# Prompt attention in pairs of query blocks, with split probabilities and values and a third probability buffer

## What is computed

```
def fox_attend_block(q, cq, qpos, k, v, ck, kpos):
    s = jnp.einsum('nqhd,nkhd->nhqk', q, k).astype(jnp.float32) * (FOX_HEAD_DIM ** -0.5)
    bias = jnp.swapaxes(cq, 1, 2)[..., :, None] - jnp.swapaxes(ck, 1, 2)[..., None, :]
    mask = kpos[None, :] <= qpos[:, None]
    p = jax.nn.softmax(jnp.where(mask, s + bias, -jnp.inf), axis=-1)
    return jnp.einsum('nhqk,nkhd->nqhd', p.astype(v.dtype), v)
```

## Time and profile before

| | |
|---|---|
| time, 3 runs | 1847.37 us median (1846.79 to 1848.72) |
| the profiled execution | 1848.54 us, its span 1846.5 us |
| PE busy over the span | 97% (PEld 93%) |
| DVE, ACT, POOL busy | 55%, 28%, 42% |
| granted PE clock, mean | 0.995 of 2.4 GHz |

### The profile page before, as it was taken

The page is one execution under the profiler, slowest core; times in us unless marked ns, Lnnn a source line. Parts: engine busy times, 40 slices in busy tenths (PEclk is TensorE's granted clock), DMA queues, the critical chain, the costliest instruction groups (busy, mean ns, idle before and its releaser), DMA issues.

```text
span 1846.5 us, 31613 instructions
## 1 busy us (share of the span) xinstructions
PE 1790.3 (97%) x11891; PEld 1716.0 (93%) x11891; DVE 1024.1 (55%) x1456; ACT 511.5 (28%) x718; POOL 772.1 (42%) x622
## 2 busy tenths in 40 slices
PE   6989999999999999999999999999999999999997
PEld 5989978788899989999999999899999999899997
DVE  6773244425633344213243479966677778766666
ACT  6111033414321122110121033444444444100012
POOL 2333210022233343334332323698889996333330
PEclk9999999999999999999999999999999999999999
DMA  5111230022222232232134421232222225422302
GB/s 154 36 47 37 51 89 24 13 64 69 63 68 68 71 95 87 58 98 75 58 92 102 135 87 47 71 103 69 69 82 79 81 69 210 151 93 93 112 0 94
DMA packets 167795, 146.10 MB, mean 79 GB/s; under 512 B 14614, under 2 KB 150651, under 8 KB 167670
## 3 DMA queue, kind: packets, MB, share of 16 engines
q1 hardware_dynamic: 163863, 131.72, 23.7%
q10 hardware_dynamic: 3841, 13.14, 1.9%
HBM read 111.59 MB, written 33.21 MB: 78 GB/s over the span
## 4 chain that ended last, share of the span: by engine, by line
PE 78%; DVE 13%; POOL 5%; ACT 2%; issue 2%; DMA 0%; ACTq 0%; POOLq 0%; SPq 0%; DVEq 0%
PE ps L2537 13%; PE ps L2543 12%; PE ps L2540 12%; PE ps L2986 5%; PE ps L3106 3%; PE ps L3112 3%; PE ps L3109 3%; DVE cv L2340 2%; PE ps L3136 2%; PE ps L2758 2%; PE pt L3136 2%; PE ps L3138 2%; PE ps L3137 2%; PE pt L3138 2%; PE pt L3137 2%
## 5 line engine op out<-in xcount | busy, mean ns | idle before, releaser
L1103 POOL TENSOR_TENSOR mark<-eps 128x1 f32<-128x1 f32 x123 | 39.8, 324 | 801.7 <-PE ps L2543 300.6
L2537 PE MATMUL ps<-h_hi,w_hi 128*128 128x352 f32 x1608 | 360.6, 332 | 3.7 <-ACT y_all L1435 2.0
L2543 PE MATMUL ps<-h_hi,w_lo 128*128 128x352 f32 x1608 | 347.2, 323 | 0.0
L2540 PE MATMUL ps<-h_lo,w_hi 128*128 128x352 f32 x1608 | 346.5, 323 | 0.0
L2537 PEld LDWEIGHTS ps<-h_hi,w_hi 128*128 128x128 f32 x1608 | 268.3, 189 | 14.6 <-issue 11.0
L2543 PEld LDWEIGHTS ps<-h_hi,w_lo 128*128 128x128 f32 x1608 | 275.8, 188 | 0.0
L2540 PEld LDWEIGHTS ps<-h_lo,w_hi 128*128 128x128 f32 x1608 | 274.0, 188 | 0.0
L1110 POOL TENSOR_TENSOR w_lo<-w_raw,w_hi 128x1024 fp32r<-128x1024 f32 x69 | 182.6, 2647 | 5.5
L2340 DVE SCALAR_TENSOR_TENSOR cv<-ext,pv,cv 128x1072 f32<-128x1072 f32 x88 | 169.4, 1925 | 9.4 <-DVE fstate L2338 2.0
L2461 DVE TENSOR_TENSOR x_acc<-x_acc,ps 128x352 f32<-128x352 f32 (+3 forms) x136 | 70.5, 518 | 43.0 <-PE ps L3138 38.8
L2461 DVE TENSOR_TENSOR x_acc<-x_acc,pt 128x352 f32<-128x352 f32 (+2 forms) x128 | 67.1, 524 | 47.3 <-PE pt L3138 44.6
(11 more groups left out here) (452 smaller groups left out, 4007.4 us busy)
## 6 DMA issues: line engine op xcount, KB each, us to landing
w_raw<-in_w_in SPq DMA_DIRECT2D x52, 512.0 KB, 4.3
w_raw<-in_ffn_up SPq DMA_DIRECT2D x26, 512.0 KB, 4.7
act_in<-act_dram SPq DMA_DIRECT2D x11, 1056.0 KB, 5.0
act_dram<-cv SPq DMA_DIRECT2D x22, 512.0 KB, 2.7
y_all<-in_ffn_up SPq DMA_DIRECT2D x18, 512.0 KB, 4.5
gates_dram<-y_all ACTq DMA_DIRECT2D x16, 528.0 KB, 2.7
cst<-gates_dram SPq DMA_DIRECT2D x16, 528.0 KB, 3.6
w_raw<-in_ffn_down SPq DMA_DIRECT2D x12, 512.0 KB, 4.0
```

The source lines that it names most:

```text
L2537: mm(dst[:, c, 0:CH], f_hi[n][:, k, :], h_hi[:, k, tok], start=k == 0, stop=False)
L2540: mm(dst[:, c, 0:CH], f_hi[n][:, k, :], h_lo[:, k, tok], start=False, stop=False)
L2543: last = mm(dst[:, c, 0:CH], f_lo[n][:, k, :], h_hi[:, k, tok], start=False, stop=k == KD - 1)
```

## The change

The 32 steps become 16 pairs (query blocks 2p and 2p+1 of a head; p 0 to 3). Units replace the groups of transposes: unit u of a pair holds key blocks 2u and 2u+1 of both query blocks (four blocks; the last unit three). A pair has p+1 units. For each unit ACT copies PSUM to `p_hi` (fp32r) and DVE subtracts it from PSUM into `p_lo` (fp32r). The value matmul has upper and lower values side by side as 128 output channels, and both query blocks as 256 columns (128 for the last key block), once with `p_hi` and once with `p_lo`. So the result has an upper half and a lower half of rows; ACT copies one half out (`low_rows_out`, word C) and DVE adds the other (`att_output`, word A). The order of all this is written out as words for each engine; a bar is a chunk of the projection. There are three `pr` buffers (the third is one of the two places of the gates, so the "ga" gates use one place), and `k_out` also carries the values out. `sdt_t` shrinks to 16 columns a block, and its transposes go in three units in place of two.

More of the change, by code:

```diff
@@ L329, in decoder_layer @@
         take(("ga", i), 1)
-    for qb in range(NT):
-        for h in range(NH):
-            take(("att", qb, h), 0)
+    pairs = [(p, h) for p in range(NT // 2) for h in range(NH)]
+    steps = [(2 * p + j, h) for p, h in pairs for j in range(2)]
+    for qb, h in steps:
+        take(("att", qb, h), 0)
     for m, j in enumerate(jobs_c):
@@ L1432, in gate_out @@
             slot_filled(act, s)
[L1433 to L1436, removed]
-        exponentials(0)
[L1439 to L1445, removed]
+            if sent >= 1:
+                act.wait_ge(g_sent[place_of], 16 * sent)
@@ new lines, in gate_out, with attention_piece @@
+            od.run(sc.activation(in_chunks(y_all[:, 6 + place_of, :]), chunked(buf(s)), ACT.Copy), free_of(s))
+            act.dma_start(gates_dram[m], y_all[:, 6 + place_of, :]).then_inc(g_sent[place_of], 16)
+        def attention_piece(word, m):
+            last = m + 1 == len(pairs)
+            if word[0] == "H":
+                probabilities_upper(m, int(word[1]))
+            elif word == "C" and m >= 1:
+                low_rows_out(m - 1)
+            elif word[0] == "E" and not last:
+                exponentials(2 * m + 2 + "ab".index(word[1]))
@@ L1447, in xbc_act @@
+        exponentials(0)
+        exponentials(1)
+        for n, (i, k) in enumerate(spots):
+            for word, m in act_groups[n - 1] if 1 <= n <= len(act_groups) else ():
+                attention_piece(word, m)
+            if k == KD - 1:
+                gate_out("ga", i)
+        for group in act_groups[len(spots) - 1:]:
+            for word, m in group:
+                attention_piece(word, m)
+        low_rows_out(len(pairs) - 1)
         def xbc_act(b):
@@ L1484, in _ @@
         free_of_sx(act)
-        od.run(sc.activation(eacs[:, :, :], sdt_t[:, :, 64:64 + NH], ACT.Exp), eacs_done)
+        od.run(sc.activation(eacs[:, :, :], sdt_t[:, :, 2 * NH:3 * NH], ACT.Exp), eacs_done)
         for c in range(NT + 1):
@@ L2146, in decays @@
             mask = const("ssdneg") if c < NT else const("blkneg", slice(0, NS))
[L2147 removed]
+            own = sdt_t[0:r, c, 2 * NH:3 * NH]
             last = bc[:, :, P - 1] if c < NT else ps[buf(s)][0:NS, 0, 256:260]
@@ new lines, in _ @@
+        pieces = {}
+        for n, spot in enumerate(spots):
+            if n == 0:
+                pieces[spot] = [lambda: scores(1)]
+            elif n <= len(groups):
+                pieces[spot] = [lambda word=word, m=m: attention_piece(word, m) for word, m in groups[n - 1]]
+        pieces.update({(0, 1): [lambda: turn_job("v", 0)], (0, 3): [lambda: turn_job("v", 1)],
+                       (0, 4): [attention_front]})
+        for i in range(NGA):
+            for piece in pieces.get((i, 0), ()):
+                piece()
+            project(N1B + i, {k: pieces.get((i, k), ()) for k in range(1, KD)})
@@ L2780, in sample_keys @@
+        for group in groups[len(spots) - 1:]:
+            for word, m in group:
+                attention_piece(word, m)
+        pe.wait_ge(att_out, len(pairs))
         def sample_keys(n):
```

213 lines of the change are left out of this document (106 added, 107 removed).

## The result

The changed kernel took **1858.7 us** (median of 4, 1857.65 to 1859.79) against 1847.14 on the same chip: ratio 1.0061, 95% interval [1.0044, 1.0078], slower by 11.6 us. The same text on another chip: 1857.81 (median of 5) against 1847.89, ratio 1.0051 [1.0037, 1.0065], slower by 9.9. The profiled execution took 1857.65 us with a span of 1854.9, so its span is 8.4 us longer than that of before and 0.7 us more lies outside it. The forecast was 1856 in 1845 to 1862. Two executions in all, one of the kernel before (2805.8 us) and one of experiment 5 (3475.5), were disturbed and are left out of the ratios.

What follows compares the result with a forecast made beforehand. PE, busy 97% of the span, bounds the kernel before; after the change the row of links sets the loop. +4.0 + 5.5 - 1.0 = +8.5 us on 1848.5 gives 1857.0 profiled, so 1856 predicted, range 1845 to 1862.

Steps and rivals of the forecast that it cites:

- The loop, +4.0: Attention loop: pair times, quicker PE starts and gate costs sum to 148.6 us against 144.6, so +4.0 us.
- Case (a): Attention loop: the forecast itself, the row of dependent links sets the loop's time; 1851 to 1861 us, chance 0.62.
- -1.3: Attention loop: PE starts sooner after a wait than in the rows, some 0.08 us a pair, -1.3 us.
- The pairs: Attention loop: each pair's length worked out from its chain of waits, 6.31 to 12.2 us, together 145.9 us.
- The links: Attention pairs: each operation's time costed from trace rows, unseen ones from similar rows; subtraction 0.69 us, output sum 0.42.
- rival (d): Attention loop: POOL blocks normalization at each gate (+6) or subtraction costs half as much again (+8); 1862 to 1865, chance 0.10.
- The saving, 22 us of PE's work: Value matmuls in attention: 12.0 us from fewer loads plus some 10 of idle time removed from PE.
- The 10 us of idle time: Before value matmuls (5.3 us) and projection loads (7.1 us "issue"): some 10 us goes, since new matmuls have 128 channels.
- Rival (b): Attention loop: PE stays the bound and the 22 us show, some 1830 us, or half, 1842; chance of either 0.14.
- Gates, 4.0: Attention loop at five gates: gate output ahead on ACT, and POOL's weight split slowing normalization (1.4 us); sum 4.0 us.
- Before the loop, +5.5 - 1.0: Values' turns delay first transposes from 232.98 to 238.5 us, +5.5; smaller sample copies in the fifth projection give -1.0.
- case (e): Attention loop: stalls bring the granted clock to 1.2 GHz; a third at half speed gives +33 us, 1890; chance 0.02.

Runs made afterwards that it cites:

- experiment 5: Changed kernel with only TensorE's first scores of each pair moved ahead of its first transposes: four executions 1855.6 to 1870.3 us, ratio to before 1.0068.
- experiment 1: Changed kernel with VectorE's first subtraction of each pair made twice: 1868.83 us, ratio to before 1.0116.
- experiment 2: Changed kernel with six more 256-column matmuls per pair ahead of TensorE's wait for scaled probabilities: 1856.4 us, ratio to before 1.0042.
- experiment 3: Kernel before the change with the same six extra matmuls every second step, at the same place: 1860.36 us against 1848.08, ratio 1.0068.
- experiment 4: Changed kernel reordered: scores ahead of transposes, maximum ahead of subtraction and output sum, exponential ahead of high copy: 1835.39 us, ratio to before 0.9935.
- experiment 9: Changed kernel with the values' transfer buffer handed back after VectorE's copy, low part computed from that copy: 1856.96 us against 1857.81.
- experiment 10: Changed kernel with the transfer buffer handed back after VectorE's copy, and sample rows copied to and stored from their own tile: 1857.64 us, ratio to before 1.0047.
- experiment 6: Changed kernel with only VectorE's and ScalarE's orders changed (maximum, exponential first), TensorE's order kept except T3 a chunk earlier at p = 3: 1872.11 us, ratio to before 1.0133.

## Why the prediction was right, by its own steps

**The loop, +4.0: measured +4.05** (148.67 against the predicted 148.6). Case (a) holds, and experiments 1 to 3 show it as cause. That the sum meets to 0.1 us is in part luck: the eleven pairs without a gate came out 1.7 us shorter than in the list below and the five with one 4.4 longer, for the -1.3 and +4.0 taken; 0.8 of the 4.4 is a fallen clock, and the second profile, without it, has a loop 0.7 us shorter. The pairs, predicted and measured: p = 0 6.31, and 5.79, 6.62, 6.29; next 7.8, and 7.71; p = 1 8.1, and 8.56, 8.02, 8.08; then 9.7, and 9.59; p = 2 9.75, and 11.18, 9.54, 9.62; then 11.3, and 11.11; p = 3 12.2, 11.4, 12.2, and 13.23, 11.22, 12.05; the last 8.85, and 10.06. The longer ones (6.62, 8.56, 11.18, 13.23, 10.06) hold a gate, the extra cost that the pair times left out; 11.18 holds a fallen clock as well (below): in the second profile that pair lasts 10.37.

**The links** were sized well, those unseen before too. Groups of the changed kernel, 228 to 388 us, beside L1425, L2021 and the 256 columns of L2033 in the earlier trace rows, which stood in for them:

```profile
L2122 DVE TENSOR_TENSOR p_lo<-pt,p_hi 128x512 fp32r<-128x512 f32 x24 | 16.6, 691 | 19.5 <-ACT p_hi L1465 19.2
...
L1465 ACT ACTIVATE p_hi<-pt 128x512 fp32r<-128x512 f32 x24 | 14.3, 598 | 27.3 <-issue 17.3 <-PE pt L2837 9.9
...
L2130 DVE TENSOR_TENSOR y_all<-ps,y_all 64x256 f32<-64x256 f32 x16 | 6.8, 422 | 4.2 <-ACT y_all L1472 3.7
```

0.69 and 0.42 us as taken: a second input from SBUF made neither slower, so rival (d) fails in that part.

**The saving, 22 us of PE's work: some 19**, seen in experiment 4. In the changed kernel itself only 14.4 shows; its busy time holds matmuls at the lower clock and, as I read it, others spread out by waits. The new matmuls with 256 columns are 0.12 apart and those with 128 columns 0.06, not the 0.1 assumed, so the loads save 13.3 us and not 12.0. The 10 us of idle time were put too high: in experiment 4 the "issue" time of the loads ahead of the projection is down from 7.1 to 0.9 us, but ahead of the value matmuls 4.5 are left of 4.9. Rival (b) was wrong for this order of words and nearly right for another: it gave 1830 where PE stays the bound; with scores first it is 1835.

**Gates, 4.0.** The lock came as the earlier trace rows let expect, at two of five gates:

```profile
308.21 1.04 POOL L1142 CAST w_hi<-w_raw 128x1024 fp32r<-128x1024 f32 x1
308.27 1.38 DVE L2114 TENSOR_SCALAR stg<-stg,ast 128x768 f32<-128x768 f32 x1
309.32 2.55 POOL L1143 TENSOR_TENSOR w_lo<-w_raw,w_hi 128x1024 fp32r<-128x1024 f32 x1
```

This multiplication takes 0.62 us alone (between 0.55 for 640 columns and 0.69 for 896) and 1.38 beside POOL's cast; another takes 0.96 where 0.49 is usual. Together 1.2 us, predicted 1.4. The subtractions from PSUM kept their length, 24 of them at a mean of 0.691 us, and so did the four of all that ran beside POOL's second instruction (L1143), two at 0.69 and two with three blocks at 0.56: as the forecast had it by the rule of the Trainium skill, "SBUF — State Buffer", section "Who interferes with whom".

**Before the loop, +5.5 - 1.0.** The first transposes came 4.9 us later (237.87 for 232.98), where 4.5 were predicted. The early part gave -0.5 and not -1.0: the wait for VectorE of the earlier trace rows became 3.2 us, the clock fell behind it all the same, and 112 to 116 us again stand at 0.50. The rest is +5.4, and 1.4 of it is the chunk that before stood in the loop, so the start itself is 4.0 us slower. The forecast took both stretches with these borders and its sum is not touched by that. In the turn, transposes and what stands between them:

```profile
222.13 1.23 ACT L1450 ACTIVATE v_split<-pt 128x512 fp32r<-128x512 f32 x2 [0.85 <-PE pt L2652]
222.86 0.69 DVE L2094 COPY k_out<-pt 128x512 f32<-128x512 f32 x1 [11.61 <-ACT v_split L1450]
...
223.58 0.69 DVE L2096 TENSOR_TENSOR v_split<-pt,v_split 128x512 fp32r<-128x512 f32 x1
...
224.33 0.28 PE L2652 MATMUL pt<-cst,stg 128*32 128x128 f32 x1 [1.86 <-DVE v_split L2096]
```

The size was right. Of the two causes given for it, copies in series and landing of stores, the copies set it here, and VectorE waited 0.3 us for a landing; in experiments 9 and 10 the landing took their place, with stores that the edits themselves made later. Which of the two would be left with an early store stays open.

**The step that was mis-sized: the granted clock, case (e).** I took it for all or nothing, a third of the work at half speed with a chance of 0.02, else zero, since "the loop's are near 1 us". It comes in small pieces. In the second profile of the changed kernel it fell right behind the turn's waits, and in the first one in the loop:

```profile
225.00:230.00 5.00, 5.00 (x25) 4.93 (x25) 1.67 (x5) 0.04 (x1) 0.00 (x0) 0.66 0.38 105
```

```profile
300.00:304.00 4.00, 4.00 (x21) 4.00 (x20) 3.47 (x7) 1.76 (x4) 0.00 (x0) 0.57 0.00 0
```

Behind the first of these the transposes of probabilities start 32.7 us after the turn of keys and not 31.2. It falls in some executions of a kernel and not in others: of the changed kernel and the variants that leave the turn alone, the profiles of four stand at 31.1 to 31.2 us (experiments 1, 4 and 6 and the first one), and of five at 32.7 to 33.1. Five of nine at 1.6 us more are some 0.9 us on average, and the forecast has no term for it. The medians lie 1.8 and 2.7 us above the 1856 predicted; in the first measurement 0.7 is the time outside the span, in the second (1.7 us outside, for 2.0 before) none. Of the rest I can only argue that it is the same thing.

## What to carry to other kernels

When a change takes work off the bounding engine, write out the row that leads from one round back to itself, with each engine's order of words in it, before counting the saving: if that row is longer than the work that is left, the saving turns into waits. Then look for links that stand there only because of an order; here the same instructions took 22 us less in another order, and only there did the change pay. Reorder all engines together, since an in-order engine puts whatever stands ahead of a link onto the row (a half gave +14 us), and measure the bound by adding work: the same matmuls cost 12, 0 and 5.6 us in three kernels whose busy shares look alike.

## What the runs showed of the hardware

- TensorE's granted clock fell behind waits of one to two microseconds, in some executions and not in others: after a wait of 1.76 us, scores took 3.78 us for 1.9, and executions of one kernel 1855.6 and 1870.3 us. In two profiles of the changed kernel the same wait of 1.40 us stands ahead of the ninth pair's transposes; behind it the clock fell in one (300 to 304 us at 0.57) and not in the other, and the pair lasts 11.18 and 10.37 us. So idle time on TensorE can cost more than its length.
- Work that fills the waits did no harm: with six extra matmuls a pair no stretch of 4 us in the loop stood below full clock, and the median was 1856.4 against 1858.7 and 1857.8. Whether it does good is not shown, since the second profile of the changed kernel has no such stretch either.
